# Two norm stages of a hybrid Hyena/SSD trunk step: the early projection thirds moved behind the last tile's transposes, and x loaded ahead of the weights

## What is computed

```python
hs = _modulate(_rmsnorm(xs, norm_g[i, 0]), sh1s, sc1s)
# layer 0, in _hyena_mixer:
u = _dwconv(h @ in_w + in_b, short_w, short_b)
# layer 1, in _ssd_mixer:
proj = h @ in_w
```

## Time and profile before

| what | value |
|---|---|
| median of 3 runs | 3720.36 us (3720.31 to 3724.67) |
| the profiled execution | 3719.02 us |
| its span in the profile | 3717.2 us |
| mean granted TensorE clock | 0.95 of full speed |
| PE (matmul) busy | 3377.8 us, 91% |
| DVE busy | 1863.2 us, 50% |
| ACT busy | 1282.5 us, 35% |
| POOL busy | 368.8 us, 10% |

### The profile page before, as it was taken

The page is one execution under the profiler, slowest core; times in us unless marked ns, Lnnn a source line. Parts: engine busy times, 40 slices in busy tenths (PEclk is TensorE's granted clock), DMA queues, the critical chain, the costliest instruction groups (busy, mean ns, idle before and its releaser), DMA issues. The chain is left out here.

```text
span 3717.2 us, 58914 instructions
## 1 busy us (share of the span) xinstructions
PE 3377.8 (91%) x24087; PEld 2910.3 (78%) x24087; DVE 1863.2 (50%) x3038; ACT 1282.5 (35%) x2056; POOL 368.8 (10%) x359
## 2 busy tenths in 40 slices
PE   5999898977699999996999999689995699999995
PEld 4999674755699999995899999556663699999995
DVE  5333487766433333333444554699996433333333
ACT  4322323232133233334433223266763133333333
POOL 0000000000111111111010000000000111111111
PEclk8999898988899999997999999899997799999998
DMA  6666313254688888884143443487776488888885
GB/s 237 225 201 202 131 47 126 104 202 173 232 292 291 288 288 287 287 288 137 54 142 107 149 150 102 165 324 252 257 238 265 161 290 287 287 287 288 288 288 188
DMA packets 414216, 799.49 MB, mean 215 GB/s; under 512 B 22039, under 2 KB 108892, under 8 KB 412763
## 3 DMA queue, kind: packets, MB, share of 16 engines
q1 hardware_dynamic: 384940, 700.50, 53.5%
q0 software_dynamic: 28928, 96.96, 8.9%
q10 hardware_dynamic: 208, 0.10, 0.0%
HBM read 688.59 MB, written 108.90 MB: 215 GB/s over the span
## 5 line engine op out<-in xcount | busy, mean ns | idle before, releaser
L2367 PEld LDWEIGHTS moe_banks<-moe_xt,mix_ring 128*128 128x128 f32 x8192 | 1011.4, 191 | 5.5 <-issue 3.2
L2367 PE MATMUL moe_banks<-moe_xt,mix_ring 128*128 128x144 f32 x8192 | 1012.7, 287 | 3.1 <-ACT moe_xt L2402 3.1
L62 PE MATMUL ssd_banks<-h_leading,ssd_w_split 128*128 128x384 f32 x1920 | 415.9, 345 | 1.5 <-DVE ssd_w_split L3033 1.5
L2447 DVE TENSOR_TENSOR moe_hid<-moe_banks,moe_sg 128x128 f32<-128x128 f32 x256 | 74.7, 292 | 580.1 <-ACT moe_sg L2425 580.1
L2389 PE MATMUL moe_banks<-moe_down_parts,moe_hid_parts 128*128 128x512 f32 x1536 | 357.6, 392 | 0.0
L62 PEld LDWEIGHTS ssd_banks<-h_leading,ssd_w_split 128*128 128x128 f32 x1920 | 338.3, 189 | 16.1 <-issue 13.6
L2389 PEld LDWEIGHTS moe_banks<-moe_down_parts,moe_hid_parts 128*128 128x128 f32 x1536 | 285.8, 188 | 71.4 <-issue 13.2
L2437 DVE TENSOR_TENSOR moe_down_parts<-mix_ring,moe_down_parts 128x2048 fp32r<-128x2048 f32 x128 | 292.2, 2283 | 0.0
L3314 PE MATMUL scan_banks<-scan_w,scan_yc 128*128 128x512 f32 x576 | 254.8, 596 | 0.0
L2334 POOL DMA_INDIRECT x_dram<-moe_yc,mix_idx_quarter x128 | 166.5, 1301 | 816.9 <-DVE moe_yc L2458 787.7
L62 PE MATMUL hyin_early_banks<-h_leading,hyin_early_w_split 128*128 128x384 f32 x1152 | 244.2, 339 | 0.9 <-PEq L100 0.9
(11 more groups left out here) (460 smaller groups left out, 4381.6 us busy)
## 6 DMA issues: line engine op xcount, KB each, us to landing
mix_ring<-in_moe_w_gate SPq DMA_DIRECT2D x64, 2048.0 KB, 8.1
mix_ring<-in_moe_w_up SPq DMA_DIRECT2D x64, 2048.0 KB, 13.0
mix_ring<-in_moe_w_down SPq DMA_DIRECT2D x64, 2048.0 KB, 9.0
early_ring<-in_ada_w SPq DMA_DIRECT2D x84, 512.0 KB, 5.8
scan_cum<-row_dram SPq DMA_DIRECT2D x36, 1024.0 KB, 6.4
ssd_w<-in_ssd_in_w SPq DMA_DIRECT2D x40, 512.0 KB, 4.2
s_dram<-ssdin_work SPq DMA_DIRECT2D x64, 256.0 KB, 3.5
scan_states<-s_dram SPq DMA_DIRECT2D x32, 512.0 KB, 7.7
```

Of the source, the lines that this page charges most:

```text
L62: ins = pe.matmul(out(piece), w_at(w[a], k), h_k(h[b], k, piece), start=(k == 0 and a == 0 and b == 0), stop=(k == KD - 1 and a == 1))
L2367: ins = pe.matmul(pb[:, 2 * (f % 2) + j, 0:SLOTS], ring[:, 2 * half + j, k, col:col + P], xt[:, k, :], start=(k == 0), stop=(k == KD - 1))
L2447: dve.tensor_tensor(hid[:, f % 2, :], up[:, 0:CAP_LAT], sg[:, f % 2, 0:CAP_LAT], ALU.mult).then_inc(s_hid, 1)
```

## The change

In both norms all four early pieces run behind the transposes of tile 8, in the order piece 0 of both weight tiles, then piece 1 of both. `project` is given the range of k as a further argument, always the whole of it. In `phase_norm` SP issues x of tiles 0 to 3 before `ssd_first`, the splits of the dt weights and of weight tile 0 go to iterations 3 and 4, and ACT begins the phase with a square root of one column, which loads the table that the root needs, and waits for it.

```diff
@@ phase_front @@
-        THIRDS_BEHIND = {5: ((0, 0),), 6: ((1, 0),), 8: ((0, 1), (1, 1))}
+        THIRDS_BEHIND = {8: [(q, piece, range(KD)) for piece in range(2) for q in range(2)]}
...
-                def project(q, piece):
+                def project(q, piece, ks):
...
-                             keep["h_parts"], third, pieces=(piece,))
+                             keep["h_parts"], third, ks, (piece,))
...
-                        for q, piece in THIRDS_BEHIND[t]:
-                            project(q, piece)
+                        for q, piece, ks in THIRDS_BEHIND[t]:
+                            project(q, piece, ks)
@@ phase_norm @@
-        LOADS_BEHIND, DT_SPLIT_AT, SPLIT_AT = 1, 1, 2
-        THIRDS_BEHIND = {5: ((None, 0),), 6: ((0, 0),), TILES - 1: ((None, 1), (0, 1))}
+        LOADS_BEHIND, DT_SPLIT_AT, SPLIT_AT = RING - 1, 3, 4
+        THIRDS_BEHIND = {8: [(q, piece, range(KD)) for piece in range(2) for q in (None, 0)]}
...
+        s_warm = m.sem("root_table_in")
...
+                act.activation(junk[:, 0:1], keep["eps"][:, 0:1], ACT.Sqrt).then_inc(s_warm, 1)
+                act.wait_ge(s_warm, 1)
                 tile_stats(0)
...
-                def project(q, piece):
+                def project(q, piece, ks):
...
-                    product3(pe, out, parts, lambda w_, k: w_[:, k, :], keep["h_parts"], third, pieces=(piece,))
+                    product3(pe, out, parts, lambda w_, k: w_[:, k, :], keep["h_parts"], third, ks, (piece,))
...
-                        for q, piece in THIRDS_BEHIND[t]:
-                            project(q, piece)
+                        for q, piece, ks in THIRDS_BEHIND[t]:
+                            project(q, piece, ks)
```

## The result

The changed kernel takes 3731.5 us (median of 11 runs, 3729.65 to 3733.48) against 3722.7 us (11 runs, 3718.12 to 3725.34) for the kernel before. The ratio is 1.0024 with a 95% interval from 1.0016 to 1.0032, so it is 8.9 us slower, between 6 and 12. The forecast was +10.2 us (3730.6) in a range from 3726.5 to 3735.0.

The account below looks back on a forecast made before the run. PE, busy for 91% of the span, was taken to end both norms, so its work behind the last tile counts. Front +7.4 and layer 1 +2.8 make +10.2 us, 3730.6 us, in a range from 3726.5 to 3735.

Parts of the forecast that it names:

- The last tile in the front: Front norm: tile 8 transposed at 75.95, 2.8 us earlier than 78.74.
- The front's end: Front norm: four thirds behind tile 8 take 18.17 us and end at 95.71 against 88.29, +7.4 us.
- x of tile 4: Layer 1 norm: the next late transfer, landing at 1749.0, between 1748.7 and 1749.9.
- The start of layer 1's thirds: Layer 1 norm: thirds start at 1773.4, 8.1 us behind the start of tile 8's statistics at 1765.3.
- Layer 1's end: Layer 1 norm: 19.14 us of thirds end at 1792.6 against 1789.76, +2.8 us.
- The rule on matmul spacing: Moved thirds: 162.5 ns per 384-column matmul against the trace's 177; by it the time is 3729.2 us.
- (a): Rival: layer 1 comes out even and the front adds 6.4 to 7.4 us, 3727 us; chance 0.16.
- (b): Rival: x of tile 4 much later, or more of the thirds at half clock, about 3734 us; chance 0.10.
- (c): Rival: faster, as early thirds held the last tile back by more than they are worth; chance 0.03.
- (d): Rival: next phase waits for something other than PE, so later thirds are hidden, 3720 us; chance 0.04.
- The early table load: Layer 1 norm: the 1.28 us load before the first x costs nothing, since ACT idles there anyway.
- The range: Whole kernel: clock and landing bounds make +8 to +13 us; with rivals (a) and (b), 3726.5 to 3735 us.

Follow-up runs that it names:

- e2: The changed kernel with the front's thirds put back early, so layer 1's change alone; median 3723.6 us, ratio 1.0002 to the kernel before.
- e3: The changed kernel with the early thirds back behind tiles 5, 6 and 8 in both norms; median 3718.3 us, ratio 0.9985 to the kernel before.
- e4: e3 without the early table load; median 3717.4 us, ratio 0.9986 to the kernel before.
- e6: e3 with a ring of 5 x buffers instead of 4; median 3715.2 us, ratio 0.9984 to the kernel before.

## Why the prediction was right

- **The last tile in the front.** Predicted 12.1 us behind tile 5 (63.86 to 75.95), measured 12.11. The chain of two evictions, two transposes and ACT's own pace was all there was.
- **The front's end.** Predicted +7.4 us, measured +7.5, +8.2 and +6.8 in three profiles against the one profile of the kernel before, and +6.7 between the means of all profiles with the same front. The agreement to 0.1 us is therefore in part luck. The first third of 5.21 us is the shortest of its five executions; the other four have 5.7 to 6.0. The steps that decided were PE's work behind tile 8 and the barrier; leaving two thirds out gave 7.7 to 8.4 us back, so that step is shown and not only argued.
- **x of tile 4.** Predicted 15.7 us behind the first issue (1733.29 to 1749.0), measured 15.7 in the first profile, 15.6 to 17.5 in all. The upper bound of 1749.9, 16.6 us, was too low by 0.9. Both transfer rates were read from single stretches of one execution.
- **The start of layer 1's thirds.** Predicted 40.1 us behind the first issue of x, measured 40.11.
- **Layer 1's end.** Predicted +2.8 us, measured +1.3 in the profile of the changed kernel. The term that was off is the first third, 6.30 us in the sum and 4.93 measured; in the second profile it took 6.28 and the norm +2.5, and the mean of four profiles is +2.5. The sum used one draw of a quantity that changes with the execution. Here the step from PE's thirds to the next phase rests on e2 against e3: the thirds alone moved the end by 6.3 us.
- **The rule on matmul spacing.** The Trainium skill (TensorE: Matmul & The Clock Gate, section "Wait — 56ns, not 53.3ns?") gives a start-to-start rule, and by it 384 columns take an estimated 162.5 ns. The trace disagrees: the changed kernel's 72 matmuls behind the first third take about 12.7 us, 176 ns each. The row was the better price.
- **The rivals.** (a) was partly at work in the first profile, where layer 1 came out 1.5 us better than forecast, by the clock and not by the landing. (b), a later x of tile 4, appeared in e3's profile (17.5 us), 1.8 us later than in the changed kernel's. (c) and (d) did not happen; leaving two thirds out speaks against (d) directly, in the front. Under (c) the 7 us for layer 1 should be 7.7 by the prediction's own terms (1781.1 to 1773.4, the thirds' start), and 7.8 were measured; the sum doesn't use that number.
- **The early table load** was costed at nothing, and with it taken out ACT still waited for x of tile 4, so it was worth nothing.
- **The range.** The bounds named for the front (+6.4 to +10.3) and for layer 1 (landing and clock together, -2.2 to +5.5) add up to +4.2 to +15.8. The +8 to +13 stated for the forecast is a narrower choice without a working. The measured 8.9 and 10.5 us lie in both.

What remains open is the residue of timing noise: 11 runs of one kernel spread over 4 to 8 us, so the profiles' lengths, not the ratios, carry the division between front and layer 1, and these scatter too, by up to 2.4 us with the same code.

## What to carry to other kernels

A block of matmuls that fills the gaps of a slower chain costs its whole length when it is moved behind the chain and the phase ends with that engine: 48 matmuls more behind the front's last tile cost 9.5 us (18.3 us of thirds against 8.7), and the chain freed of them returned only 2.8, less 0.8 for transposes at half clock. Cut such filler to the length of a gap: halves of 2.2 us fitted and whole thirds of 4.2 us did not, which the lengths show and the times alone do not. When transfers are reordered, look for the first one behind the block that was passed (here x of tile 4), since it takes over the wait, and an edit in front of that wait, such as an earlier table load, buys nothing until it is gone.

## What the runs showed of the hardware

The clock can fall back inside a gap that it survived in other executions. In the layer-1-only kernel, whose front is that of the kernel before, the last tile was transposed at half clock, and 48 matmuls behind it took 9.54 us instead of 8.72; the whole front took 27.8 us instead of 25.4. Its last transposes in the front, from PE's timeline, and its stretches there, all engines (columns as in rows 4):

```profile
78.57 1.94 PE L372 MATMUL hyin_early_banks<-tri,hyena_work 128*128 128x128 f32 x8 [1.99 <-ACT front_h L301]
```

```profile
76.00:78.00 2.00, 0.57 (x6) 0.33 (x4) 1.05 (x3) 1.39 (x5) 0.00 (x0) 1.00 0.00 0
78.00:80.00 2.00, 1.43 (x7) 1.47 (x8) 0.56 (x1) 1.41 (x3) 0.00 (x0) 0.64 0.00 0
80.00:82.00 2.00, 2.00 (x9) 2.00 (x8) 1.63 (x4) 1.45 (x5) 0.00 (x0) 0.51 0.00 0
```

PE was busy for 0.57 of the 2 us before the fall. In the old kernel's profile the same gap of 1.99 us before tile 8 passed at full clock, and so it did in the other three profiles with this front (e3, e4, e6). Of the 2.4 us, 0.8 are the first third (6.04 us against 5.21) and the rest comes from this fall. The halves leave no such gap; whether that is part of why they did better than expected was not tried by itself.
